# Reading the split expert weights from the last column to the first, and filling the output bank backwards

## The reference

```python
def moe_ffn(x, w_r, wg, wu, wd):
    xt = x.reshape(-1, D)
    logits = jnp.dot(xt, w_r, preferred_element_type=F32)
    top_v, top_i = lax.top_k(logits, TOP_K)
    w = jax.nn.softmax(top_v, axis=-1)
    gates = jnp.einsum('tk,tke->te', w, jax.nn.one_hot(top_i, N_EXPERTS, dtype=F32))
    for e in range(N_EXPERTS):
        h = jax.nn.silu(xt @ wg[e]) * (xt @ wu[e])
        y = y + gates[:, e:e + 1] * jnp.dot(h, wd[e], preferred_element_type=F32)
```

## Time and profile before

| | |
|---|---|
| time, median of 3 runs | 1535.76 us (1535.21 to 1536.22) |
| span of the profiled execution, first to last instruction | 1535.8 us |
| the same execution's own time | not listed apart from the three above |
| TensorE busy | 1527.8 us, 99% |
| VectorE, ScalarE, GpSimd busy | 1234.4, 998.9 and 217.5 us |
| matmuls | 8428 |
| moved by DMA | 437 MB, 285 GB/s over the span |

### The profile page before, as it was taken

The page is one execution under the profiler, slowest core; times in us unless marked ns, Lnnn a source line. Parts: engine busy times, 40 slices in busy tenths (PEclk is TensorE's granted clock), DMA queues, the critical chain, the costliest instruction groups (busy, mean ns, idle before and its releaser), DMA issues.

```text
span 1535.8 us, 21611 instructions
## 1 busy us (share of the span) xinstructions
PE 1527.8 (99%) x8428; PEld 1333.0 (87%) x8428; DVE 1234.4 (80%) x1253; ACT 998.9 (65%) x1079; POOL 217.5 (14%) x249
## 2 busy tenths in 40 slices
PE   9999999999999999999999999999999999999998
PEld 7989999999998988888888888888888888888887
DVE  5877666654477758988988888998998988898897
ACT  5655433333466547777777778777777777777775
POOL 5514400001150403101001001002002002002000
PEclk9999999999999999999999999999999999999999
DMA  8333455444443459999999999999999999999994
GB/s 226 96 110 116 149 164 164 133 157 151 125 122 110 141 209 367 383 366 388 372 381 376 374 374 376 391 359 386 384 363 382 381 362 379 400 361 363 394 373 183
DMA packets 159701, 437.43 MB, mean 285 GB/s; under 512 B 12068, under 2 KB 66176, under 8 KB 145264
## 3 DMA queue, kind: packets, MB, share of 16 engines
q1 hardware_dynamic: 151796, 423.02, 75.0%
q0 software_dynamic: 5552, 9.62, 2.3%
q10 hardware_dynamic: 2252, 3.41, 0.7%
HBM read 429.40 MB, written 13.60 MB: 288 GB/s over the span
## 4 chain that ended last, share of the span: by engine, by line
PE 98%; DMA 0%; ACT 0%; DVE 0%; issue 0%; SPq 0%; DVEq 0%; ACTq 0%
PE bank L1981 34%; PE bank L2475 13%; PE bank L2484 13%; PE bank L2479 13%; PE bank L2510 6%; PE bank L2513 6%; PE bank L2519 6%; PE bank L1984 3%; PE bank L2528 2%; PE bank L2496 0%; PE bank L2502 0%; PE bank L2495 0%; DMA gla<-b_g 0%; DVE x L1972 0%; ACT L1076 0%
## 5 line engine op out<-in xcount | busy, mean ns | idle before, releaser
L1808 DVE TENSOR_TENSOR split_lo<-raw,split_hi 128x2048 fp32r<-128x2048 f32 x336 | 763.1, 2289 | 101.8 <-ACT split_hi L1207 100.8
L1207 ACT CAST split_hi<-raw 128x2048 fp32r<-128x2048 f32 x336 | 640.5, 1911 | 224.5 <-PE bank L2484 145.7
L2475 PE MATMUL bank<-split_hi,xgT_hi 128*128 128x512 f32 x896 | 291.7, 395 | 0.0
L2479 PE MATMUL bank<-split_hi,xgT_lo 128*128 128x512 f32 x892 | 285.8, 390 | 0.0
L2484 PE MATMUL bank<-split_lo,xgT_hi 128*128 128x512 f32 x896 | 239.9, 390 | 0.0
L913 ACT CAST cut_hi<-ring 128x1024 fp32r<-128x1024 f32 x124 | 129.9, 1048 | 166.6 <-PE bank L1981 166.6
L1981 PE MATMUL bank<-xT_hi,cut_hi 128*128 128x320 f32 x752 | 236.7, 315 | 0.0
L1981 PE MATMUL bank<-xT_hi,cut_lo 128*128 128x320 f32 x752 | 233.5, 310 | 0.0
L1981 PE MATMUL bank<-xT_lo,cut_hi 128*128 128x320 f32 x752 | 231.9, 308 | 0.0
L1346 DVE TENSOR_TENSOR cut_lo<-ring,cut_hi 128x1024 fp32r<-128x1024 f32 x124 | 153.0, 1235 | 80.7 <-ACT cut_hi L913 79.9
L2484 PEld LDWEIGHTS bank<-split_lo,xgT_hi 128*128 128x128 f32 x896 | 168.3, 188 | 34.9
(11 more groups left out here) (316 smaller groups left out, 1723.2 us busy)
## 6 DMA issues: line engine op xcount, KB each, us to landing
raw<-moe_w_gate SPq DMA_DIRECT2D x112, 1024.0 KB, 7.8
raw<-moe_w_up SPq DMA_DIRECT2D x112, 1024.0 KB, 7.6
raw<-moe_w_down SPq DMA_DIRECT2D x112, 1024.0 KB, 7.3
ring<-w_in SPq DMA_DIRECT2D x15, 1024.0 KB, 5.5
ring<-ffn_w_gate SPq DMA_DIRECT2D x11, 1024.0 KB, 5.5
ring<-ffn_w_up SPq DMA_DIRECT2D x11, 1024.0 KB, 5.4
ring<-ffn_w_down SPq DMA_DIRECT2D x10, 1024.0 KB, 5.1
ring<-w_out SPq DMA_DIRECT2D x8, 1024.0 KB, 5.0
```

Source lines behind the costliest of these rows:

```text
L1207: return nc.scalar.copy(split_hi[:, i % SR, :], raw_piece(i)).then_inc(hi_ready, 1)
L1808: V.tensor_tensor(split_lo[:, i % SR, :], raw_piece(i), split_hi[:, i % SR, :].bitcast(F32), ALU.subtract).then_inc(lo_ready, 1)
L2475: TE.matmul(o, xgT_hi[:, kk, :], hi[:, w * k + 512 * c:w * k + 512 * c + 512], start=kk == 0, stop=False)
L2479: TE.matmul(o, xgT_lo[:, kk, :], hi[:, w * k + 512 * c:w * k + 512 * c + 512], start=False, stop=False)
```

## The change

A helper `back` is added that reverses the last axis of the output and of the moving operand. Column 511 is read first and written to place 511 of the bank, column 0 last. All lines of `experts` that multiply with a piece call it in place of the matmul; arguments, order, waits and signals are the same.

```diff
+            def back(out, lhsT, rhs, start, stop):
+
+                return TE.matmul(out[:, ::-1], lhsT, rhs[:, ::-1], start=start, stop=stop)
+
             def experts(count, ip, first=False):
...
-                                TE.matmul(o, xgT_hi[:, kk, :], hi[:, w * k + 512 * c:w * k + 512 * c + 512], start=kk == 0, stop=False)
+                                back(o, xgT_hi[:, kk, :], hi[:, w * k + 512 * c:w * k + 512 * c + 512], start=kk == 0, stop=False)
...
-                                last = TE.matmul(o, xgT_hi[:, kk, :], lo[:, w * k + 512 * c:w * k + 512 * c + 512], start=False, stop=kk == KB - 1)
+                                last = back(o, xgT_hi[:, kk, :], lo[:, w * k + 512 * c:w * k + 512 * c + 512], start=False, stop=kk == KB - 1)
...
-                                TE.matmul(banks[6 + n][:], hmT_hi[:, b, :], hi[:, c], start=b == 0, stop=False)
+                                back(banks[6 + n][:], hmT_hi[:, b, :], hi[:, c], start=b == 0, stop=False)
```

More of the change, by code:

```diff
@@ L2478, in experts @@
                             for c, o in enumerate(outs):
-                                TE.matmul(o, xgT_lo[:, kk, :], hi[:, w * k + 512 * c:w * k + 512 * c + 512], start=False, stop=False)
+                                back(o, xgT_lo[:, kk, :], hi[:, w * k + 512 * c:w * k + 512 * c + 512], start=False, stop=False)
                         pe.wait_ge(lo_ready, ip * (2 * NP) + (i + 1 + PR))
@@ L2488, in experts @@
                                 for c, o in enumerate(outs):
-                                    last = TE.matmul(o, xgT_lo[:, k, :], hi[:, w * k + 512 * c:w * k + 512 * c + 512], start=False, stop=False)
+                                    last = back(o, xgT_lo[:, k, :], hi[:, w * k + 512 * c:w * k + 512 * c + 512], start=False, stop=False)
                     elif q == NP - 1:
@@ L2494, in experts @@
                                 c = slice(1024 * k + 512 * n, 1024 * k + 512 * n + 512)
-                                TE.matmul(banks[6 + n][:], hmT_hi[:, b, :], hi[:, c], start=False, stop=False)
-                                TE.matmul(banks[6 + n][:], hmT_lo[:, b, :], hi[:, c], start=False, stop=False)
+                                back(banks[6 + n][:], hmT_hi[:, b, :], hi[:, c], start=False, stop=False)
+                                back(banks[6 + n][:], hmT_lo[:, b, :], hi[:, c], start=False, stop=False)
                             if n == 0:
@@ L2501, in experts @@
                                 c = slice(1024 * k + 512 * n, 1024 * k + 512 * n + 512)
-                                last = TE.matmul(banks[6 + n][:], hmT_hi[:, b, :], lo[:, c], start=False, stop=k == 1)
+                                last = back(banks[6 + n][:], hmT_hi[:, b, :], lo[:, c], start=False, stop=k == 1)
                             if n == 0:
@@ L2518, in experts @@
                                 c = slice(1024 * k + 512 * n, 1024 * k + 512 * n + 512)
-                                last = TE.matmul(banks[6 + n][:], hmT_hi[:, b, :], lo[:, c], start=False, stop=b == FEB - 1)
+                                last = back(banks[6 + n][:], hmT_hi[:, b, :], lo[:, c], start=False, stop=b == FEB - 1)
                     last.then_inc(piece_used, 1)
```

## The result

The changed kernel takes 1561.98 us (median of 4 runs, 1561.2 to 1562.6) against 1535.61 us for the kernel before on the same chip: a ratio of 1.0166, 95% interval 1.0153 to 1.0179. That is 26.4 us more. It lies in the stated range, 1533 to 1592 us, but it is not the forecast case of no change; it lies where the first rival stood, with a smaller surcharge. About 2 us of the 26.4 are probably not the change's: all four runs of the changed kernel have a mean granted clock of 0.997, at which the kernel before took 1537.2 us or more in the later experiments, against 1535.1 to 1536.0 us at 0.999 or 1.000; and the two profiled executions, both at 0.997, differ by 24.2 us.

The account below looks back on a forecast made before the run. TensorE was taken to bound the kernel, its 4032 expert products filling 914 of 955.5 us busy in that stretch. At 4032 x 0 ns added, the forecast stayed at 1535.8 us, range 1533 to 1592 us.

Parts of the forecast that it names:

- the forecast case of no change: Experts' products: a reversed product costs 0 ns more, time stays 1535.8 us; chance 0.66.
- the first rival: Fixed start per reversed product, columns at full pace: 4032 x 11.5 ns = 46 us, 1582 us; decides from 0.8 ns; chance 0.13.
- What bounds the kernel: Experts' stretch: TensorE busy 955.5 of 959.8 us; 1 ns per product is 4.0 us, other engines give no cover.
- Nothing for instructions, waits and transfers: Whole kernel: no instructions, waits or DMAs added, removed or moved by the change; cost 0.
- Span and median taken for one number: Profiled span 1535.8 us and median 1535.76 us taken as the same, with nothing between them to add.
- The forward pace: Forward products: 0.420 ns per column plus 11.5 ns per product, from 226.7 ns at 512 and 146 ns at 320 columns.
- The price of the order: Experts' products: reversed column order costs between 0 and 256 ns per product; 0 taken.
- the read of hm: Transposes' stationary operand, every fourth float: load 204 against 140 ns, 64 ns more over 128 columns; taken as price of distance.
- The argument by neighbourhood for the bank: Bank write: a step of -1 stays as near as +1, so backward writing costs 0, though no row exists.
- Half the pace: Second rival, experts' products: backward columns at half pace, 427 ns a product, 807 us more, 2343 us; chance 0.15.
- the full price of a far column: Third rival: every backward column pays 0.5 ns more, 1032 us in all, 2568 us; chance 0.04.
- The fourth rival: Program builder turns the mirrored product round again: 1535.8 us; no chance of its own, inside that for no change.

Follow-up runs that it names:

- turned fours: Changed kernel, but only the read altered: groups of four neighbours taken last to first, ascending inside, write forward: 1561.78 us, ratio 1.0158 to the kernel before.
- forward halves: Each 512-column product of the experts made into two of 256 columns, all forward: 1587.03 us, ratio 1.0325 to the kernel before.
- four blocks: Changed kernel, but only the read altered: four blocks of 128 columns taken last to first, ascending inside, write forward: 1537.26 us, ratio 1.0000.
- backward halves: Two products of 256 columns for each of 512, each read backward and written forward: 1575.20 us, ratio 1.0248 to the kernel before.

## Why the prediction was right and where it was not

**What bounds the kernel: right.** TensorE alone, no cover, so that a surcharge per product counts 4032 times. The spans show 24.2 us, 6.0 ns each. (4032 x 6.6 = 26.6 us, so near the 26.4 us of the medians, is a chance agreement: the one leaves out the slower forward products behind transposes, the other holds the 2 us or so of clock.) That the other engines would only wait more also held: ScalarE's idle time before its casts went from 224.5 to 249.3 us, VectorE's before its subtractions from 101.3 to 124.3 us.

**Nothing for instructions, waits and transfers: right.** Counts, the first 576 us and the other engines' busy times are unchanged.

**Span and median taken for one number: wrong, and harmless.** The execution with the span of 1535.8 us is none of the three that were timed. In every run whose span is recorded the time is 1.7 to 1.9 us above it (1561.8 and 1560.0 for the changed kernel), so that the profiled execution took about 1537.6 us, and 1535.76 us belongs to executions at a slightly higher mean clock. The mix-up is worth under 2 us.

**The forward pace: nearly right.** With the forward halves, 106.7 ns over 256 columns are 0.417 ns a column and leave 13.3 ns on top, where the prediction had 0.420 and 11.5 from products of two stages.

**The price of the order, "between 0 and 256 ns I take 0": wrong.** This is the step that failed. It took the read of hm for a price of distance and argued that a step of -1 is as near as +1, four columns in the same 16 bytes either way. Two things are wrong in it. The price of the hm read is not one of distance: a step of 2, half as far and with two columns in 16 bytes, costs 224 ns a product where a step of 4 costs 234. And the argument about four columns in either order, while true (the turned fours cost nothing), leaves out the order in which the fours are visited, which is where the 6.6 ns are: 233.3 ns with the groups descending, 226.7 ns with them ascending. The prediction looked inside the four and not from one four to the next.

**The argument by neighbourhood for the bank: the value right.** The write had no row at all and is free in reverse. The Trainium skill's rule that "any non-contiguous AP slows matmuls significantly" ("PSUM — Partial Sum Buffer", Specifications) does not reach to a step of -1: 226 ns. Larger steps in the bank were not run.

**The first rival: the right place for a wrong reason.** Its sum was 4032 x 11.5 = 46 us, 1582 us; the size is 6.6 instead of 11.5. Its mechanism, a fixed start per product with the columns at full pace, is refuted by the sizes (+0.9 ns at 320 columns, -1.7 at 256); the four blocks and the turned fours speak against it too. The straight line through the sizes says the opposite, slower columns and a smaller part besides them, but it is argued, not shown, as long as the weight loads may have a part in the two smaller sizes. What in TensorE makes a descent cost stays open. The forward product's 11.5 ns was taken for something that a gain could hardly touch; the backward halves show that some of it can go.

**Half the pace, and the full price of a far column: excluded here.** Products of about the length that these two rivals had (427 and some 480 ns) do exist, 451 and 461 ns, but with steps of 2 and 4. They have nothing to do with direction.

**The fourth rival, a mirrored product turned back into a forward one: refuted,** since the time moved, and reading alone reversed moves it as much.

**The chances.** 0.66 on no change was too much for an argument from a single row, which by the prediction's own words could not tell its two readings apart, and from no row for the write. That the range nevertheless held the time is luck: it was stretched upward for the first rival, whose mechanism the runs refute, and the true surcharge happened to fall inside.

## What to carry to other kernels

For float32 matmuls like these, one weight load to each, the write side can run backward for free at 512 columns, and the read side can take four neighbours in descending as in ascending order; what costs on the read side is a step of 2 or 4 (twice the time) and, slightly, descending from group to group (3% at 512 columns, under 1% at 320, a small gain at 256). Directions should not be mixed from product to product without need. Where one product's surcharge is multiplied by thousands on the engine that sets the end, a price without a row should not be set to zero because it looks like its neighbour: 0.8 ns a product was the point of decision here, and no argument from a 64 ns row resolves that.

## What was not expected of the hardware

- A moving operand of 512 floats read with a step of 2 costs 451 ns, almost the 461 ns of a step of 4; unit steps of either sign cost 227 to 233 ns.
- A step of -4 costs 473 ns, 12 ns more than +4, while -1 costs 6.6 ns more than +1: there is no single price for descending.
- Backward reads of 256 columns start 118.3 ns apart, forward ones 120.0 ns, and the gain is in every other product (119.6 and 117.0 ns in turn).
- Moving columns in groups of four neighbours, each group descending, pass at full pace: 226.7 ns for 512.
- After backward products the next two forward ones are still slow (0.47 us for the two, then 0.45).
